# Two feed-forward networks: gate and up matmuls issued for two PSUM banks in turn

## What is computed

```python
def swiglu(x, w_gate, w_up, w_down):
    return (jax.nn.silu(x @ w_gate) * (x @ w_up)) @ w_down
...
        f = swiglu(rms_norm(h, ffn1_pre_g[i]), ffn1_w_gate[i], ffn1_w_up[i], ffn1_w_down[i])
        h = h + 0.5 * rms_norm(f, ffn1_post_g[i])
        m = hybrid_mixer(rms_norm(h, mix_pre_g[i]), w_in[i], rpb[i], pool_w[i], pool_scale[i],
                         w_br_attn[i], w_br_pool[i], w_out[i])
        h = h + rms_norm(m, mix_post_g[i])
        f = swiglu(rms_norm(h, ffn2_pre_g[i]), ffn2_w_gate[i], ffn2_w_up[i], ffn2_w_down[i])
        h = h + 0.5 * rms_norm(f, ffn2_post_g[i])
```

## Time and profile before

| | |
|---|---|
| median of 3 runs | 2140.82 us |
| lowest, highest | 2140.75, 2143.81 us |
| profiled execution, span | 2141.4 us |
| TensorE busy | 2108.3 us, 98% |
| TensorE weight loads busy | 1737.8 us, 81% |
| DVE, ACT, GpSimd busy | 883.8, 785.1, 884.7 us |
| HBM read, written | 192.41 MB, 2.10 MB |
| gate and up of the first network, from the first up to the last | 1061 to 1356 us |
| the same of the second | 1733 to 2028 us |

### The profile page before, as it was taken

How to read it: one execution, slowest core, us unless ns; L and a number is a source line. 1 busy time by engine, 2 the same in 40 slices (tenths; PEclk the granted TensorE clock), 3 DMA queues, 4 the chain that set the end, 5 groups by cost and what they waited for, 6 DMA issues and landing times.

```text
span 2141.4 us, 33679 instructions
## 1 busy us (share of the span) xinstructions
PE 2108.3 (98%) x13932; PEld 1737.8 (81%) x13932; DVE 883.8 (41%) x1621; ACT 785.1 (37%) x1606; POOL 884.7 (41%) x688
## 2 busy tenths in 40 slices
PE   8999999999999999999999999999999999999998
PEld 7878887778978888778888888888888888888876
DVE  6074564525365464535532212443422622222264
ACT  4423324445423235455422222244523432222244
POOL 4543433232443433232454544443444445454433
PEclk9999999999999999999999999999999999999999
DMA  6422223122221222112242332233132133332222
GB/s 243 166 75 80 77 67 99 40 79 61 98 81 60 95 67 88 51 60 89 70 134 73 118 99 98 89 114 99 60 118 99 59 99 108 108 104 95 98 69 89
DMA packets 98680, 196.67 MB, mean 92 GB/s; under 512 B 3680, under 2 KB 12256, under 8 KB 98144
## 3 DMA queue, kind: packets, MB, share of 16 engines
q1 hardware_dynamic: 95072, 183.25, 26.0%
q10 hardware_dynamic: 3456, 11.27, 1.5%
HBM read 192.41 MB, written 2.10 MB: 91 GB/s over the span
## 4 chain that ended last, share of the span: by engine, by line
PE 61%; DVE 5%; ACT 2%; issue 0%; DMA 0%; DVEq 0%; ACTq 0%
PE ps L876 18%; PE ps L877 18%; PE ps L878 18%; DVE work L1953 1%; DVE xs L1945 1%; DVE work L1934 1%; PE ps L985 1%; PE ps L996 1%; PE ps L1064 1%; PE ps L1005 1%; PE ps L1147 0%; DVE xl L1969 0%; PE ps L988 0%; DVE side L1598 0%; PE ps L1167 0%; ACT work L1486 0%
## 5 line engine op out<-in xcount | busy, mean ns | idle before, releaser
L825 POOL TENSOR_TENSOR wl<-raw,wh 128x512 fp32r<-128x512 f32 (+2 forms) x684 | 884.5, 1317 | 1231.8 <-ACT wh L1222 1221.5
L1222 ACT CAST wh<-raw 128x512 fp32r<-128x512 f32 (+2 forms) x692 | 380.4, 603 | 762.8 <-PE ps L878 661.4
L876 PE MATMUL ps<-xh,wh 128*128 128x512 f32 (+1 forms) x1376 | 514.6, 374 | 1.2 <-issue 1.2
L878 PE MATMUL ps<-xh,wl 128*128 128x512 f32 (+1 forms) x1376 | 508.9, 370 | 0.0
L877 PE MATMUL ps<-xl,wh 128*128 128x512 f32 (+1 forms) x1376 | 508.4, 369 | 0.0
L876 PEld LDWEIGHTS ps<-xh,wh 128*128 128x128 f32 x1376 | 259.3, 188 | 46.6 <-issue 3.9
L878 PEld LDWEIGHTS ps<-xh,wl 128*128 128x128 f32 x1376 | 259.0, 188 | 44.7
L877 PEld LDWEIGHTS ps<-xl,wh 128*128 128x128 f32 x1376 | 259.3, 188 | 42.0
L876 PE MATMUL ps<-wh,xh 128*128 128x512 f32 (+1 forms) x608 | 239.1, 393 | 0.2 <-issue 0.2
L878 PE MATMUL ps<-wh,xl 128*128 128x512 f32 (+1 forms) x608 | 234.4, 386 | 0.0
L877 PE MATMUL ps<-wl,xh 128*128 128x512 f32 (+1 forms) x608 | 234.3, 385 | 0.0
(11 more groups left out here) (257 smaller groups left out, 2424.4 us busy)
## 6 DMA issues: line engine op xcount, KB each, us to landing
raw<-w_in SPq DMA_DIRECT2D x58, 1024.0 KB, 5.2
raw<-w_out SPq DMA_DIRECT2D x20, 1024.0 KB, 5.0
raw<-f1g SPq DMA_DIRECT2D x10, 1024.0 KB, 5.1
raw<-f1u SPq DMA_DIRECT2D x10, 1024.0 KB, 5.1
raw<-f1d SPq DMA_DIRECT2D x10, 1024.0 KB, 5.1
raw<-f2g SPq DMA_DIRECT2D x10, 1024.0 KB, 5.1
raw<-f2u SPq DMA_DIRECT2D x10, 1024.0 KB, 5.1
raw<-f2d SPq DMA_DIRECT2D x10, 1024.0 KB, 5.0
```

The costliest lines, as they stand in the source:

```text
L825: pool.tensor_tensor(wl[s], raw[:, u % 2, k, 0:b.width], wh[s].bitcast(F32), ALU.subtract).then_inc(low_done, 1)
L876: pe.matmul(o, still[0], move[0], start=k0 + k == 0, stop=False)
L878: mm = pe.matmul(o, still[1], move[0], start=False, stop=k0 + k == b.ktiles - 1)
L1222: act.copy(wh[:, v % 3, k, 0:width], raw[:, v % 2, k, 0:width]).then_inc(high_done, 1)
```

## The change

In `plan`'s loop on TensorE, a block that is evacuated by `silu` or `times_gate` (gate or up of a feed-forward network) and is not begun is now issued in pairs of pieces, by a new function:

```diff
+            def piece_pair(pa, pb):
...
+                b, unit, j = pa
+                u = b.unit_ids[unit]
+                _, k0, nk = units[u]
+                oh, ol = operand[b.operand]
+                if k0 == 0:
+                    if j == 0:
+                        if b.need[0] == "evac":
+                            wait(pe, dve_evac, b.need[1])
+                        else:
+                            wait(pe, act_step, b.need[1][1])
+                            wait(pe, dve_step, b.need[1][2])
+                    for n in (j, j + 1):
+                        if b.prior[n] is not None:
+                            pb_, pj = b.prior[n]
+                            pe.wait_ge(act_evac if pb_.engine == "act" else dve_evac, pb_.evacs[pj])
+                for k in range(nk):
+                    if j == 0:
+                        pe.wait_ge(low_done_dve if low_on_dve(u, k) else low_done, low_at[u, k])
+                    last = k0 + k == b.ktiles - 1
+                    for w, m, first, stop in ((wh, oh, k0 + k == 0, False), (wh, ol, False, False), (wl, oh, False, last)):
+                        mms = [pe.matmul(ps[:, b.bank(n), :], w[:, u % 3, k, n * P:(n + 1) * P], m[:, k0 + k, :],
+                                         start=first, stop=stop) for n in (j, j + 1)]
+                for n, mm in zip((j, j + 1), mms):
+                    if b.ends(pa):
+                        mm.then_inc(bank_ready, 1)
+                    elif n == b.banks - 1:
+                        mm.then_inc(unit_done, 1)
...
             for e in plan:
-                if isinstance(e, Block):
+                if isinstance(e, Block) and e.evac in ("silu", "times_gate") and not e.begun:
+                    pieces = e.pieces()
+                    for n in range(0, len(pieces), 2):
+                        piece_pair(pieces[n], pieces[n + 1])
+                elif isinstance(e, Block):
                     for pc in half_pieces(e, 1) if e.begun else e.pieces():
                         piece(pc, half=1 if e.begun else None)
```

## The result

The changed kernel takes 2155.07 us (median of 4 runs, 2151.82 to 2155.79), the kernel before 2142.12 in the same session; the ratio is 1.006, with a 95% interval of 1.0048 to 1.0071. In a second session, with five and fifteen runs, the ratio is 1.0066 (1.0053 to 1.0078). It is slower, by 0.5 to 0.8%. The forecast was 2151.8 us in a range of 2144 to 2158, so the measured median lies inside the range, 3.3 us above the forecast. The profiled execution took 2151.82 us, with a span of 2150.0.

What follows compares the result with a forecast made beforehand. TensorE, busy 98% of the span, bounds the kernel. Matmul distance changes by zero; A 1.8, B 0.9, C 2.4 and restarts 0.4 make 5.5 us per FFN, twice 11.0, giving 2151.8 us, range 2144 to 2158.

Steps and rivals of the forecast that it cites:

- Distance between matmuls: Start-to-start time of the 1920 moved matmuls: claimed unchanged at 226.7 ns, a change of zero.
- The 13 ns: 13.4 ns per 512-column matmul beyond 213.3 ns for columns; rival blaming same-bank accumulation forecast 2131.3 us, chance 11%.
- The three places: Places in each FFN where TensorE would wait for banks: 5.5 us per FFN with restarts, 11.0 us in all.
- The reserve of 0.8 us: Up of the 256-wide chunk: products through after 7.4 us, down wants bank 1 after 8.2, so no wait.
- A: Gate of the 256-wide chunk into its up: first matmul waits for both silus, 1.8 us plus 0.1 restart.
- hand-over: Delay from a bank's release to TensorE's start, taken as 0.04 us.
- B: Down of chunk 0 into gate of chunk 2: first pair waits for bank 1's copy, 0.9 us plus 0.1 restart.
- C: Up of chunk 2 into down of chunk 1: waits for banks 2 and 3, 2.4 us plus two 0.1 us restarts.
- T: Reference time at place C, 1169.91 us in the trace of before, when both banks' products were to start.
- 0.7 us for C without GpSimd: Place C without GpSimd in the way: bank 3 done at T + 4.9, C's sum 0.7 us, time 2148.4 us.

Runs made afterwards that it cites:

- covered pairs: Changed kernel with single pieces at the three waiting places, 1632 of 1920 matmuls still in pairs: 2141.37 us, ratio 0.9996 to the kernel before.
- all pairs: The changed kernel itself, run again beside the follow-up kernels: 2155.91 us, against 2142.88 for the kernel before.
- the early release: Changed kernel, but a bank of an up counts as free after the first of VectorE's three operations: 2153.37 us, ratio 1.0054.
- the quiet GpSimd: Changed kernel, GpSimd's eight subtractions for the first network's chunk 3 gate weights cut to one column each: 2151.77 us, one run.
- the narrow split: Changed kernel with single pieces in the 256-wide chunk: gate's last unit in the first network, up's first unit in the second; 2152.40 us, one run.
- the shifted kernels: Kernel before, front SBUF tile 32 bytes smaller, 80 smaller, 32 larger, shifting nearly all tiles: 2141.28, 2144.14, 2143.51 us, one run each.
- exchanged parts: Kernel before with the product tile pairs exchanged: chunks 0, 2, 4 write zh and zl, chunks 1, 3, 5 yh and yl; 2142.35 us, one run.

## Why the prediction was right, step by step

**Distance between matmuls, taken as unchanged: right.** Changing the bank with every matmul gave and cost nothing, by the durations, the 5.44 us of a pair, and the covered pairs. The 13 ns above the time of the columns do not hang on the bank. The Trainium skill (TensorE: Matmul & The Clock Gate, "Back-to-back issue gap") gives 215.8 ns, by the formula that it offers for a matmul taken alone, and about 131 ns for a stream of weight loads and matmuls of 512 columns. These fp32r matmuls, each with a weight load, start every 226.7 ns, in pairs as in single pieces, so the trace agrees with neither.

**The three places: right,** with their releasers and in both networks, and no other place came up. The reserve of 0.8 us in the up of the narrow chunk held.

**A: 1.8 us and 0.1 predicted, 2.0 and 0.08 measured.** The times of the silus were right (the second ends 1.74 us after the point at which the up should start; I had 1.77). The step that was too small is the hand-over, 0.04 us from a row of the attention; here the matmul starts 0.26 us after the silu's end (1093.85 to 1094.11). **B: 0.9 and 0.1 predicted, 1.14 and 0.08 measured,** for the same reason: 0.26 us from 1127.74 to 1128.00. At C, where one wait stands ahead of the matmul, the hand-over is 0.06 us. At A and B further waits of TensorE stand behind the one that ends last; that they make the 0.2 us was not tried.

**C: 2.4 and 0.2 predicted, 1.7 and 0.2 measured.** The mechanism stood, GpSimd's part in it too. Two sizes were off: bank 2's chain began 0.04 us ahead of T, and the cast beside GpSimd took 0.80 us, not the 1.09 of the earlier trace rows. So bank 3 was free at T + 5.9, not T + 6.6. The prediction's 0.7 us for C without GpSimd was wrong: it took the slowing out of bank 3's chain alone, though bank 2's subtraction of 1.67 us is slowed as well. With GpSimd cut short all of C went.

The sum, 11.0 predicted and 10.4 read from the trace, was right partly because A and B, too small, and C, too large, cancelled: that part is luck. So is the forecast's agreement with the profiled execution (2151.8 and 2151.82 us), and the median of 2155.07 fell into the range because the range was wide, not because it had a term for what follows.

**What was missing: the clock.** The medians differ by 13 us, the places explain 10.4. In the profiled execution of all pairs that took 2155.74 us, place A of the second network is followed by this (table of stretches: before the wait, the first matmuls behind it, the next, and after):

```profile
1766.00:1771.80 5.80, 5.80 (x27) 4.67 (x25) 0.00 (x0) 1.67 (x6) 4.22 (x6) 1.00 0.82 239
1773.90:1775.20 1.30, 1.30 (x6) 1.08 (x7) 0.00 (x0) 1.08 (x3) 0.78 (x2) 1.00 0.05 13
1775.40:1778.60 3.20, 3.20 (x9) 2.53 (x8) 0.00 (x0) 0.91 (x2) 3.20 (x4) 0.50 0.98 310
1778.80:1784.00 5.20, 5.20 (x25) 4.29 (x24) 0.00 (x0) 2.19 (x4) 3.04 (x3) 1.00 0.57 187
```

TensorE was busy, idled for 1.84 us, started again at full clock, and some 1.5 us later the granted clock is 0.50 (1.2 GHz). Eight matmuls start every 427 ns in place of 227: 1.6 us lost. The traces of after, all pairs, the early release and the quiet GpSimd hold eight such places, and the clock falls behind three of them. It does not behind the shorter waits, here or in the narrow split (0.74 and 0.89 us idle). So A costs 2.1 us in some executions and 3.7 in others, twice over. That makes up to 3.2 us more and covers the 2.6 us that are missing, though the traces are too few to say how often it happens. It was no term of my sum.

The wait at 46 us behaves alike. Seven of the fourteen traces have it at 1.82 to 2.18 us, before and all pairs among them, and in all seven the clock falls behind it; the other seven have it at 0.23 to 0.65 us, after among them, and in none does it fall. Of the kernels whose matmul distances are those of the kernel before, the profiled executions with this fall took 2143.15 to 2144.14 us (the covered pairs, the second and third of the shifted kernels), the four without it (the first of the shifted kernels, the two that move `zh` and `zl`, the one with exchanged parts) 2140.86 to 2142.35. That fits the two clusters of times of the kernel before (2140.4 to 2141.4 and 2142.5 to 2144.5), and it gives a second reading of the change: the profiled execution of after, which has no fall at either place, took 2151.82 us, 9.5 to 11.0 more than those four without one. The three places make 10.4.

## What to carry to other kernels

Interleaving two accumulations doubles the time from first to last matmul of a bank and makes two banks fall due together. It is free where two evacuations fit behind the pair, so look at the blocks with the fewest banks and at every change of block for the ones that do not. A wait has more in it than its length: what the releasing engine owes next (at C an earlier release moved four fifths of the wait one block on), and the clock that may fall behind a long one. Where neighbouring matmuls into one bank and into different ones stand at the same distance in the trace, alternating banks has nothing to win.

## What the runs showed of the hardware that I had not expected

A single TensorE wait of about 2 us, between stretches without other idle time, can be followed by half the granted clock. From 20 to 2100 us the fourteen traces hold 178 waits of 0.6 to 1.5 us, and the clock never fell behind one. They hold 15 longer ones: behind the eight of 1.84 us it fell in three cases, 0.8 to 1.5 us after TensorE had started again; behind the seven of 1.82 to 2.18 us at 46 us it fell each time. It fell nowhere else in that time. No run changed such a wait alone, so that the wait brings the fall on is argued from these counts. At the lower clock a matmul of 512 columns takes 427 ns, just its columns at 1.2 GHz: the 13 ns of the full clock are not paid there. The Trainium skill (TensorE: Matmul & The Clock Gate, "Wait — 56ns, not 53.3ns?") says the same of its smaller extra time, and the traces agree on that point.

Where a tile lies in SBUF relative to the tile it is multiplied with seems to set 226.7 or 233.3 ns for the same matmul, which made 29 us of 2141 when the most used operand was moved. GpSimd's subtractions make a VectorE cast of 0.43 us last 0.80 us (1.09 and 1.32 in the earlier trace rows) and a subtraction of 0.69 us last 1.65; with GpSimd cut short at the same place, both are back at 0.43 and 0.69.
